# VectorE makes every low part of the weights, every low part of y and the square sums of layers 0 and 1

## The reference, cut to what matters

```
mod  = silu(c) @ ada_w[l] + ada_b[l]          # and the same with c_ctx for the context tokens
h    = rmsnorm(x, norm_g[l]) * (1 + scale) + shift
fnet:  y = (fft2(h).real * silu(h @ w_gate)) @ w_out
mlstm: q, k, v, o, g, z = split(h @ w_in)     # 8 heads, two directions
       y = (rmsnorm(sigmoid(o) * h_scan, hn) * silu(z)) @ w_out
attn:  q, k, v, z = split(h @ w_in);  y = (attend(q, k, v) * silu(z)) @ w_out
x    = x + gate * y
```

## Time and profile before

| | us |
|---|---|
| median of 3 runs | 3490.86 (3487.54 to 3492.56) |
| the profiled execution | 3491.52 |
| its span | 3489.8 |
| TensorE busy | 3348.0 (96%), granted clock 0.981 on the mean |
| VectorE busy | 2213.5 (63%) |
| ScalarE busy | 1294.3 (37%) |
| GpSimd busy | 1583.4 (45%) |

### The profile page before, as it was taken

One profiled execution on the slowest core, in us unless ns is written; L12 is line 12 of the kernel. 1 busy time (PEld: TensorE's weight loads), 2 busy tenths in 40 slices (PEclk: granted clock), 3 DMA queues, 4 the chain that ended last, 5 costly groups with the idle time before them and its releaser, 6 DMA issues.

```text
span 3489.8 us, 45164 instructions
## 1 busy us (share of the span) xinstructions
PE 3348.0 (96%) x18024; PEld 2796.5 (80%) x18024; DVE 2213.5 (63%) x3362; ACT 1294.3 (37%) x2000; POOL 1583.4 (45%) x796
## 2 busy tenths in 40 slices
PE   8899997999999999999999999999999999999999
PEld 3577686778888888787777798998999888889889
DVE  6899899788888776766578734447344554332333
ACT  3321223423222222324355544444444444443443
POOL 1143475544454444466666532444444234444443
PEclk9999998999999999999999999999999999999999
DMA  8666565344444445375577654456543345555555
GB/s 312 218 233 216 170 230 194 127 157 141 155 169 151 149 151 171 127 265 175 194 248 256 213 180 138 163 189 220 189 137 134 126 141 180 187 184 185 189 181 173
DMA packets 188707, 638.45 MB, mean 183 GB/s; under 512 B 21536, under 2 KB 31904, under 8 KB 188496
## 3 DMA queue, kind: packets, MB, share of 16 engines
q1 hardware_dynamic: 135072, 449.39, 38.2%
q10 hardware_dynamic: 51264, 180.38, 15.4%
q0 software_dynamic: 2160, 5.79, 0.6%
HBM read 622.89 MB, written 10.49 MB: 181 GB/s over the span
## 4 chain that ended last, share of the span: by engine, by line
PE 82%; DVE 10%; DMA 2%; ACT 2%; issue 2%; POOL 1%; SPq 0%; ACTq 0%; DVEq 0%; POOLq 0%
PE PS L367 15%; PE PS L369 15%; PE PS L368 15%; PE PS L418 5%; PE PS L419 5%; PE PS L420 5%; PE PS L928 3%; PE PS L930 3%; PE PS L929 3%; DVE WR L1670 2%; PE PS L616 2%; DMA WR<-ada_w 2%; DVE JUNK L1670 2%; PE PS L396 1%; POOL WL L2653 1%
## 5 line engine op out<-in xcount | busy, mean ns | idle before, releaser
L2653 POOL TENSOR_TENSOR WL<-WR,WH 128x1024 fp32r<-128x1024 f32 x530 | 1373.6, 2596 | 1672.5 <-ACT WH L1024 1671.6
L1024 ACT ACTIVATE WH<-WR 128x1024 fp32r<-128x1024 f32 x753 | 793.6, 1059 | 1289.3 <-PE PS L369 742.1
L367 PE MATMUL PS<-HTH,WH 128*128 128x256 f32 (+1 forms) x3360 | 1104.4, 329 | 28.0 <-DVE HTL L1618 19.3
L369 PE MATMUL PS<-HTH,WL 128*128 128x256 f32 (+1 forms) x3360 | 1087.5, 324 | 0.0
L368 PE MATMUL PS<-HTL,WH 128*128 128x256 f32 (+1 forms) x3360 | 1087.2, 324 | 0.0
L367 PEld LDWEIGHTS PS<-HTH,WH 128*128 128x128 f32 x3360 | 644.5, 192 | 102.3 <-issue 21.1
L368 PEld LDWEIGHTS PS<-HTL,WH 128*128 128x128 f32 x3360 | 644.8, 192 | 50.9 <-issue 3.5
L369 PEld LDWEIGHTS PS<-HTH,WL 128*128 128x128 f32 x3360 | 644.2, 192 | 48.8
L1648 DVE TENSOR_TENSOR WL<-WR,WH 128x1024 fp32r<-128x1024 f32 x223 | 292.3, 1312 | 400.2 <-ACT WH L1024 398.6
L418 PE MATMUL PS<-WH,HTH 128*128 128x512 f32 x1024 | 415.7, 406 | 20.2 <-POOL WL L2653 11.3
L420 PE MATMUL PS<-WH,HTL 128*128 128x512 f32 x1024 | 402.2, 393 | 0.0
(11 more groups left out here) (344 smaller groups left out, 3449.1 us busy)
## 6 DMA issues: line engine op xcount, KB each, us to landing
WR<-ada_w SPq DMA_DIRECT2D x320, 512.0 KB, 4.8
WR<-e_gu SPq DMA_DIRECT2D x128, 512.0 KB, 4.1
WR<-m_vo ACTq DMA_DIRECT2D x64, 512.0 KB, 4.0
WR<-a_qz ACTq DMA_DIRECT2D x64, 512.0 KB, 4.7
WR<-n_m SPq DMA_DIRECT2D x64, 512.0 KB, 3.9
WR<-e_d SPq DMA_DIRECT2D x64, 512.0 KB, 4.7
AR<-ada_p SPq DMA_DIRECT2D x48, 512.0 KB, 6.3
WR<-f_gate ACTq DMA_DIRECT2D x32, 512.0 KB, 4.9
```

The costliest lines, as they stand in the source:

```text
L367: e.matmul(ps[:, 0:n], wh[:, k, :], xh, start=c == 0, stop=False)
L369: i = e.matmul(ps[:, 0:n], wl[:, k, :], xh, start=False, stop=c == K - 1)
L1024: e.activation(WH[:, s % NP, :], WR[:, plan["slot"][p], :], ACT.Copy, scale=1.0).then_inc(*L.up(hi_done, ("hi", s)))
L2653: e.tensor_tensor(WL[:, s % NP, :], WR[:, plan["slot"][plan["split"][s]], :], WH[:, s % NP, :].bitcast(F32), ALU.subtract).then_inc(*L.up( ...
```

## The change

VectorE makes the low part of every piece, in one counter `lo_done`. GpSimd's stream loses `cut_to`, `along`, `keep_up`, `split_y` and `square_sum`; it keeps the norms' halves, the triangles, M_O, the pooling and its loads. VectorE's `split_y` does all 16 blocks in place of two of three. VectorE adds the squares of layers 0 and 1 too, three columns behind, and ScalarE's lag there becomes 2. The keys `wide`, `dve` and `pool` of the plan go. In attention, the lows of the first query pieces are made ahead of the keys of the token blocks 0 and 1.

```diff
@@ VectorE, cut_to
-                if not lo_on_pool(s):
-                    w.wait_ge(L.at(("hi", s)))
-                    e.tensor_tensor(WL[:, s % NP, :], WR[:, plan["slot"][plan["split"][s]], :],
-                                    WH[:, s % NP, :].bitcast(F32), ALU.subtract).then_inc(
-                        *L.up(lo_dve_done, ("lo", s), ("wfree", plan["split"][s])))
+                w.wait_ge(L.at(("hi", s)))
+                e.tensor_tensor(WL[:, s % NP, :], WR[:, plan["slot"][plan["split"][s]], :],
+                                WH[:, s % NP, :].bitcast(F32), ALU.subtract).then_inc(
+                    *L.up(lo_done, ("lo", s), ("wfree", plan["split"][s])))
@@ VectorE, modnorm
-            cut_to(plan["first"][tag] + NP)
+            cut_to(plan["first"][tag] + (2 if tag == 0 else NP))
@@ VectorE, split_y
-            if n % 3 != 2:
-                a, b = cols
-                w.wait_ge(L.at(("yh", tag, n)))
-                tt(HL_[:, n, a:b], YT[:, n, a:b], HHF[:, n, a:b], ALU.subtract, ("ys", tag, n))
+            a, b = cols
+            w.wait_ge(L.at(("yh", tag, n)))
+            tt(HL_[:, n, a:b], YT[:, n, a:b], HHF[:, n, a:b], ALU.subtract, ("ys", tag, n))
@@ VectorE, square_sum and outproject
-            r, x = (RS, SQR[n % 2]) if tag == 3 else (RA, SQR[n % 2][:, 0:256])
+            r, x = (RS, SQR[n % 2]) if tag in (0, 1, 3) else (RA, SQR[n % 2][:, 0:256])
...
-                if n >= 2 and tag in (2, 3, "nsa"):
-                    square_sum(tag, n - 2)
+                lag = 3 if tag in (0, 1) else 2
+                if n >= lag:
+                    square_sum(tag, n - lag)
...
+            if tag in (0, 1):
+                square_sum(tag, 13)
@@ ScalarE, outproject
-            lag = 3 if tag in (0, 1) else 1
+            lag = 2 if tag in (0, 1) else 1
@@ VectorE, attn
+            s0 = plan[("qz", 0)][0]
+            cut_to(s0 + 1 + NP)
             for tb in (0, 1):
@@ VectorE, the start
-        cut_to(NP - 1)
         fnet(0, "x0", 0, ALL)
@@ GpSimd
-        def cut_to(n):
...
-                if lo_on_pool(s):
-                    w.wait_ge(L.at(("hi", s)))
-                    e.tensor_tensor(WL[:, s % NP, :], WR[:, plan["slot"][plan["split"][s]], :],
-                                    WH[:, s % NP, :].bitcast(F32), ALU.subtract).then_inc(
-                        *L.up(lo_pool_done, ("lo", s), ("wfree", plan["split"][s])))
...
-        cut_to(NP - 1)
-        fnet(0, ALL)
+
+        modnorm(0, ALL)
         mlstm()
         attn()
```

More of the change, by code:

```diff
@@ L131, in _program @@
         "vc", "ks", "kw", "moe")}
-    every = [mm_done, hi_done, act_done, lo_dve_done, lo_pool_done, dve_done, ada_done, pool_done,
+    every = [mm_done, hi_done, act_done, lo_done, dve_done, ada_done, pool_done,
              x_stored, out_stored, *w_landed, *adap_landed, *adaw_landed, *x_landed, *const_landed.values()]
@@ L137, in _program @@
     plan = {"src": [], "split": [], "raw": {}, "slots": [], "slot": [], "before": {}, "held": {}, "first": {},
-            "slot4": {}, "ada": [], "sp": [], "ring": None, "wide": 0, "dve": set(), "pool": set(), "done": False, "ready": False}
+            "slot4": {}, "ada": [], "sp": [], "ring": None, "done": False, "ready": False}
     SQR = [AR[:, NAR - 512 * (i + 1):NAR - 512 * i] for i in range(2)]
@@ L268, in segments @@
         return [(s, v) for s, v in ((CTX, 1), (LAT, 0)) if cols[0] <= s[0]]
-    def lo_on_pool(s):
-        return s not in plan["dve"] and (s < plan["wide"] or s % 2 == 1 or s in plan["pool"])
     def F_ORDER():
@@ L2644, in load @@
                 e.dma_start(o, I[source]).then_inc(*L.up(const_landed[name], name))
-        def cut_to(n):
-            while cut[0] < min(n, len(plan["split"])):
-                s = cut[0]
-                cut[0] += 1
-                if lo_on_pool(s):
-                    w.wait_ge(L.at(("hi", s)))
-                    e.tensor_tensor(WL[:, s % NP, :], WR[:, plan["slot"][plan["split"][s]], :],
-                                    WH[:, s % NP, :].bitcast(F32), ALU.subtract).then_inc(
-                        *L.up(lo_pool_done, ("lo", s), ("wfree", plan["split"][s])))
[L2657 to L2670, removed]
         def modnorm(tag, cols):
-            cut_to(plan["first"][tag] + NP)
             if len(segments(cols)) == 2:
                 for j in range(NB):
-                    keep_up(tag, j)
                     m = 2 * j + 1
@@ L2680, in modnorm @@
                         *done(("h", tag, j), ("hm", tag, m)))
[L2682 to L2695, removed]
         load("ident", (IDN[:], "ident"))
@@ L2707, in gpsimd_program @@
         load("ct0", (F_CT, "dft_t"))
[L2709 to L2722, removed]
         def mlstm():
@@ L2744, in mlstm @@
                             *done(("pa", h, k, d)))
[L2745 to L2753, removed]
                 if h < 7:
                     vo(h + 1)
[L2756 to L2760, removed]
         def attn():
@@ L2789, in nsa @@
             w.wait_ge(*(L.at(("h", "nsa", j)) for j in range(NB)))
-            along(("first", "nsa"))
             for i in range(2):
@@ L2832, in pool @@
                     *done(("pl", n), ("pooled", n)))
-            fill = N_FILL()
-            def go(n):
-                for _ in range(n):
-                    if fill:
-                        kind, *x = fill.pop(0)
-                        if kind == "merge":
-                            along(("n_m", x[1], x[0]))
-                        elif kind == "pool":
-                            pool(*x)
-            go(2)
             w.wait_ge(L.at(("rope", "kc2"), ("full", ("gtr",)), "masks"))
@@ L2848, in nsa @@
                 e.memset(x[:, 0:16], 0.0).then_inc(*done("pw0"))
-            for tb in range(2):
-                go(2)
-            for h in range(16):
-                go(2)
-                go(1)
-                if h % 4 == 0:
-                    go(1)
-            go(99)
-            for n in range(NB):
-                split_y("nsa", n, LAT)
-            outproject("nsa", 256)
+            for n in range(8):
+                pool(n)
         def moe():
@@ L2863, in moe @@
             load("moe", (E_RB, "r_b"), (E_IDX, "idx4"))
-            along(("gu", 0, 0))
-            for half in range(2):
-                for x in range(8 * half, 8 * half + 8):
-                    along(("gu", x, 0 if x else 4))
-                for n in range(NB):
-                    along(("out", half, "moe", n))
-        cut_to(NP - 1)
-        fnet(0, ALL)
+        modnorm(0, ALL)
         mlstm()
@@ L2876, in gpsimd_program @@
         load("ct3", (F_CT, "dft_t"))
-        fnet(3, LAT)
+        modnorm(3, LAT)
         nsa()
@@ L2977, in place_pieces @@
             plan["first"][tag] = plan[job][0]
-            if tag in (0, 3):
-                plan["dve"].update((plan[job][0] + NP, plan[job][0] + NP + 1))
-        plan["dve"].update(range(plan[("out4",)][0], plan[("dft", 3)][0], 2))
         here, newest = {}, {}
@@ L2983, in place_pieces @@
         moe_first = plan["split"][plan[("gu", 0, 0)][0]]
-        plan["pool"].update(range(plan[("gu", 0, 4)][0], plan[("gu", 1, 0)][2]))
         for p, ring in enumerate(plan["slots"]):
```

13 lines of the change are left out of this document (1 added, 12 removed).

## The result

The changed kernel takes 3604.55 us, median of 4 runs (3602.07 to 3608.09), against 3489.2 before (4 runs beside it): a ratio of 1.033 [1.031, 1.035], 115 us more. The forecast was +182 (3674, range 3580 to 3780): slower, as forecast, and inside the range, with 63% of the amount. The profiled execution spans 3605.1 us, 115.3 more than before.

A forecast was written before the change was run, and what follows sets the result against it. TensorE, busy 96% of 3489.8 us, was taken to set the time. Terms 109 + 26 + 22 + 12 + 7 + 18 - 14 + 2 = +182 on 3491.5 gave 3674 us, range 3580 to 3780.

The forecast's parts named there:

- Heads: mLSTM heads 0 to 6: bg(5) moves behind the last V/O low, TensorE idles, then runs slow; +109 us (57 to 141).
- V/O of head 0: Before head 0's V/O pieces: TensorE waits 30 us for lows behind scans and eight half blocks; +26 us (15 to 34).
- Gates: Layer 0's 14 gates: VectorE's turn of 14.85 us exceeds TensorE's 12.91; +22 us (0 to 40).
- Columns of layer 0: Layer 0's output columns: VectorE needs 14.75 us against TensorE's 10.9 in columns 0 to 5; +12 us net (0 to 23).
- Layer 1: Layer 1's output columns, where only one product is left to a half block: +7 us (0 to 15).
- attention's start: Attention's two bg(6), 13.8 us each, behind along(av) and along(ak), partly covered by idle time; +18 us (0 to 28).
- Given back: Waits on GpSimd's low parts go and VectorE operations in attention's loop are no longer stretched: -14 us (-50 to 0).
- a sign of being wrong: The forecast would be wrong if heads' period stays, products stay at 2.0 us, or waits sit in NSA and MoE.
- VectorE's bill: VectorE's busy time: 2213 + 647 for lows - 362 for shorter products + 33 = 2531 us, 72 to 73%.
- The lock is gone and the lows fit: Rival: every TensorE wait that names GpSimd goes, giving 3441 us; bg(5) must fit in 5 us at L2030; 7%.
- The products stay long: Rival: the 2.0 us products come from the DMAs, not GpSimd, so they stay long; 3747 us; 11%.
- the hold is covered: Rival: TensorE has other columns to run at L2030, so only gates, columns and the start remain; 3520 us; 5%.

The follow-up runs named there:

- x1_wait: Kernel before, with one wait added between along((vo, h + 1)) and bg(5) for the last V/O high part, no work added: 3584.55 us, ratio 1.028.
- x2_heads: Changed kernel, with bg(5)'s half blocks done one by one between the V/O low parts in heads 0 to 6: 3525.04 us.
- x8_gate: Changed kernel, with one useless VectorE product of 128 x 1024 added in each of gates 0 to 13 of layer 0: 3633.74 us.
- x7_sums: Kernel before, with VectorE adding the squares of layers 0 and 1 and ScalarE's lag of 2; GpSimd keeps its low parts: 3496.82 us, ratio 1.0016.
- x6_attn_pool: Changed kernel, with GpSimd again making the low parts of attention's query and gate pieces, but for the loop's first pieces: 3624.81 us.
- x4: Changed kernel, half blocks and lows woven in heads 0 to 6, ahead of head 0's V/O columns and in attention's keys: 3483.17 us, ratio 0.998.
- x5: x4 with layer 0's output columns alternating 3 and 2 half blocks and three low parts made before the router's chain: 3478.47 us, ratio 0.997.

## Why the prediction was right, and where its sizes were off

**The mechanism held.** The page let the change pass as free (VectorE at 73%), and the argument went by order: a low is a wait, and bg(5) moves behind it. x1_wait shows that the wait alone costs 93 us; x2_heads that the same work, woven in the heads alone, costs 34 (3525.04 against 3491.49 beside it). The spot was right, seven waits before L596. The row waited for was not the forecast's: it is the gated product (L1623) and not the copy (L1626 here, L1630 before). The forecast read the z matmul at 896.10 as one that follows the copy at once. In that trace TensorE has work without a gap up to it:

```profile
893.62 1.98 PE L593 MATMUL PS<-AR,IDN 40*128 40x512 f32 x4
895.53 1.12 PE L599 MATMUL PS<-AR 128*128 128x512 f32 x2
```

Both rows stand behind bg(5), so the size hardly changes by it.

**Heads, 109 forecast, 87.5 measured.** Two terms were too large. The seven waits are 67.6 us, forecast 79: bg(5) took 15.3 us (919.77 to 935.10), forecast 16.2, and why the wait is another 0.7 shorter is open. The clock was put at 4.3 for each gap, 30 in all, by a row of the kernel before; here the slow stretch was 5 us and cost 2.1, some 16 in all. The rest is six waits of 0.6 us at L613 (3.5 together), which the forecast did not have. After 29 us without work the slow stretch was no longer: half speed from 680.78 to 684.8, granted clock 0.76 over the 8 us.

**V/O of head 0, 26 forecast, 20.8 measured.** The wait was called as 30 us behind 655.3 and came as 29.16 up to this row:

```profile
680.78 0.80 PE L415 MATMUL PS<-WH,HTH 128*128 128x512 f32 x1 [29.16 <-DVE WL L1643]
```

The clock took 2 and not 4.3. Up to here the lead has grown by 27.8 us; behind the V/O matmuls 7.0 of them come back, since the kernel before waits there for 5.7 us (L593, for a copy of VectorE) and then runs slow. That the forecast put the sum 5 us higher is the clock for 2 of them; the other 3 I can't divide.

**Gates, 22 forecast, -1 measured.** Two terms of the step failed. One is VectorE's turn, 14.85, with "bg(3) 2.6 + 5.5 + 2.6 = 10.7" in it. The 5.5 was one reload, read from one pair of rows. The median of the 43 loads of `ada_w` between 176 and 384 was 4.6 from issue to landing, in the same trace, and 4.0 after the change. With 4.0, bg(3) is 9.2, and L1623 and L1614 of the gate take 1.4 in place of 1.7: 13.0 for a plain gate, 13.9 measured as the mean with the few longer ones. The other is TensorE's gate, 12.91: that is one gate without the work between some of them, and the mean over the stage is 13.7. The difference that was to be 1.95 a gate is 0.2. x8_gate shows that the stage was indeed close: 1.2 us more a gate, and it is VectorE's.

**Columns of layer 0, 12 forecast, -3 measured.** Three pieces make the -3. In the columns themselves the lead grows by 11.2 us; forecast 23, and with the reload of 4.0 a column with three half blocks is 13.3 in place of 14.75, which gives 14. At norm 1 the changed kernel gets 9.1 back, forecast 11: the kernel before waits 8.2 us there for VectorE's tail. And ahead of the first column it gains 5.2, which the forecast did not have: TensorE waits there for the low parts of y, 4.3 us in place of 7.26, and then runs slow for a shorter time. Over the whole kernel these waits, the largest line of the earlier trace rows with 19.3 us, fell to 11.6 (L364 on L1614). In x1_wait and x7_sums, where GpSimd keeps its low parts, they stay at 19.1 and 19.2. No run tells whether it is the division of `split_y` or the missing low parts of GpSimd beside it.

**Layer 1, 7 and -1; attention's start, 18 and 25.** In layer 1 the columns cost 4.6 us, near the 7, and the same shorter waits ahead of the first column give 5.4 back, so the near zero is two terms that cancel. In attention I counted 12 us of idling as cover. But the first bg(6) also stands ahead of the keys' lows, with a wait of 6.7, and the second ahead of the query pieces' lows, with one of 11.5; I had looked at the copies alone.

**Given back, -14 and -13.** The size was right, and the place is attention's loop (-13.8), 11 us of it by x6_attn_pool. Six of the eleven waits of L418 on a low of GpSimd lay in it, between 1812 and 1978, of 0.4 to 2.2 us and 6.8 together; the norms' waits on GpSimd (8.5 us twice after the change, 7.3 before) did not get shorter. Behind the loop the changes nearly cancel, and the forecast of 0 there is right by luck: at the router a wait of 10.8 us, where there was one of 4.2 on GpSimd, costs 5 net, in the mixture of experts, where a wait was named as a sign of being wrong.

**VectorE's bill.** 2531 forecast, 2342 measured. Lows +624 and products -359 were right (647 and -362). Missing were 170 us, nearly all of them time that came back on VectorE's other operations; I had counted the stretch on the products alone. Compared group by group, those with two SBUF inputs got 127 us shorter (64 of 128x256, HTL<-AR,MOD,HTH, went from 828 to 540 ns), TENSOR_SCALAR with one SBUF input 29 us (64 of AR<-AR,SML from 624 to 349 ns), and those with an input in PSUM not at all (YT<-PS,SML 419 and 418 ns). By the Trainium skill, "SBUF — State Buffer", section "Who interferes with whom", a VectorE instruction with two SBUF inputs contends with a GpSimd instruction that reads SBUF. The trace agrees, and this sentence should have made me count them all; the 29 us are outside this sentence.

**The total.** All terms down to layer 1 were too high, by 75 us together, attention's start was too low by 7, and 1 us less was given back. The 115 lie inside the range since it was wide, not since errors cancelled; inside single stages (columns, layer 1, what lies behind the loop) they did.

**The rivals.** "The lock is gone and the lows fit" (3441) failed at the place named: bg(5) had 5 us and needed 15.3. "The products stay long" is out by the groups after, "the hold is covered" by the seven waits. In x4 and x5, where the order is mended, the kernel ends 8 and 12 us under the kernel before, so the new division of work gave no more than that, and not 50.

## What to carry to other kernels

When work moves to an engine with time to spare, look at what it makes that engine wait for, and at what stands behind it in the queue: the 35% of idle time on VectorE did not help the gated product that came 10 us late for TensorE. Background work behind a paced series of waits belongs between its members, one unit to each, not ahead of it or behind it as a block: same instructions, 80 us less. And two durations that decide a bound are to be read over their whole stage, with all the work that lies in it, not from one row: for a gate that is VectorE's 13.9 against TensorE's 13.7, where single rows gave 14.85 against 12.91.

## What was not expected of the hardware

After an idle stretch of 10 us and after one of 29 us the slow matmuls (pitch 0.43 in place of 0.23) lasted 5 and 4 us, and in the kernel before some 8 after 7 us with a short wait among them; a longer gap did not cost more clock. VectorE's TENSOR_SCALAR of one SBUF input (AR<-AR,SML, 128x256) took 624 ns before and 349 with GpSimd nearly still. The loads of `ada_w` landed after 4.0 us in place of 4.6 in the gate stage, and 4.5 in place of 5.3 in the columns of layer 0 (median issue to landing). Part of it is spread between runs: x1_wait, whose gates are those of the kernel before, has 4.3 in the gate stage. And x7_sums has 4.6 in the columns with GpSimd's low parts in place, so these need not be the cause. No run here tells why.
